# Two transformer blocks on one core: six raw weight buffers and five pairs of split ones instead of eight and four

## What is computed

```
x = first_block(x, ...)     # rms_norm; h @ w_in; three attentions; branches; w_out; MLP
x = second_block(x, ...)    # two layers over 256 tokens and 256 context tokens

# first_block
h = rms_norm(x, norm_mix)
(q, k, v of nsa, swa and moba, merge_gate) = split(h @ w_in)
o_a = nsa_attention(..., cmp_pos, cmp_w1, cmp_w2, bias)   # compressed, selected, window
o_b = banded_attention(..., swa_sinks)
o_c = moba_attention(...)
x = x + sum(sigmoid(merge_gate) * (branches @ w_branch)) @ w_out
h = rms_norm(x, norm_mlp)
x = x + square(relu(h @ w_mlp_in)) @ w_mlp_out

# second_block, for each of two layers
shift, scale, gate = split(silu(c) @ w_mod + b_mod)       # and the same of the context
u = (rmsnorm(x) * (1 + scale) + shift) @ w_in
x = x + gate * ((attentions(u) * silu(u_gate)) @ w_o)
```

## Time and profile before

| | us |
|---|---|
| three runs | 2912.19, 2914.12, 2914.35 |
| their median | 2914.12 |
| the profiled execution | 2914.6 |
| its span | 2912.8 |
| TensorE busy (PE) | 2882.0 |
| VectorE busy (DVE) | 1985.7 |
| ScalarE busy (ACT) | 1272.7 |
| GpSimd busy (POOL) | 225.5 |

### The profile page before, as it was taken

The page is one execution under the profiler, slowest core; times in us unless marked ns, Lnnn a source line. Parts: engine busy times, 40 slices in busy tenths (PEclk is TensorE's granted clock), DMA queues, the critical chain, the costliest instruction groups (busy, mean ns, idle before and its releaser), DMA issues. The chain is left out here.

```text
span 2912.8 us, 36839 instructions
## 1 busy us (share of the span) xinstructions
PE 2882.0 (99%) x13834; PEld 2378.1 (82%) x13834; DVE 1985.7 (68%) x2768; ACT 1272.7 (44%) x2101; POOL 225.5 (8%) x303
## 2 busy tenths in 40 slices
PE   9999999999999999999999999999999999999998
PEld 7898788888888888888888878777888888878877
DVE  6897466668879999999975844544534655676655
ACT  5443355553454444443555233333433325345543
POOL 1000000011002001010100000001000100112000
PEclk9999999999999999999999999999999999999999
DMA  8988956568768878878864744334333743776444
GB/s 288 296 306 275 330 163 192 152 202 284 253 212 275 281 263 283 279 252 291 274 211 138 230 154 139 123 116 135 116 125 123 250 162 109 260 225 212 133 136 154
DMA packets 307853, 612.07 MB, mean 210 GB/s; under 512 B 25916, under 2 KB 81689, under 8 KB 306781
## 3 DMA queue, kind: packets, MB, share of 16 engines
q1 hardware_dynamic: 288268, 545.79, 57.8%
q0 software_dynamic: 18176, 62.61, 6.0%
q10 hardware_dynamic: 1232, 1.33, 0.1%
HBM read 568.98 MB, written 41.84 MB: 210 GB/s over the span
## 5 line engine op out<-in xcount | busy, mean ns | idle before, releaser
L507 DVE TENSOR_TENSOR w_lo<-raw,w_hi 128x1024 fp32r<-128x1024 f32 (+3 forms) x778 | 934.2, 1213 | 266.5 <-ACT w_hi L501 260.7
L501 ACT ACTIVATE w_hi<-raw 128x1024 fp32r<-128x1024 f32 (+3 forms) x778 | 805.2, 1047 | 697.7 <-PE acc L737 536.9
L737 PE MATMUL acc<-w_hi,a_hi 128*128 128x512 f32 (+3 forms) x2024 | 785.4, 389 | 0.6 <-ACT stage L850 0.5
L737 PE MATMUL acc<-w_hi,a_lo 128*128 128x512 f32 (+3 forms) x2024 | 778.2, 385 | 0.0
L724 PE MATMUL acc<-w_hi,a_hi 128*128 128x512 f32 (+2 forms) x1328 | 538.0, 405 | 3.9 <-DVE w_lo L507 3.7
L737 PE MATMUL acc<-w_lo,a_hi 128*128 128x512 f32 (+3 forms) x2024 | 527.2, 385 | 0.0
L726 PE MATMUL acc<-w_hi,a_lo 128*128 128x512 f32 (+2 forms) x1328 | 517.9, 390 | 0.0
L725 PE MATMUL acc<-w_lo,a_hi 128*128 128x512 f32 (+2 forms) x1328 | 516.5, 389 | 0.0
L737 PEld LDWEIGHTS acc<-w_hi,a_hi 128*128 128x128 f32 x2024 | 380.0, 188 | 75.1 <-issue 3.3
L737 PEld LDWEIGHTS acc<-w_lo,a_hi 128*128 128x128 f32 x2024 | 378.2, 188 | 72.7
L737 PEld LDWEIGHTS acc<-w_hi,a_lo 128*128 128x128 f32 x2024 | 380.1, 188 | 70.0
(11 more groups left out here) (416 smaller groups left out, 2496.2 us busy)
## 6 DMA issues: line engine op xcount, KB each, us to landing
raw<-in_w_mod SPq DMA_DIRECT2D x192, 512.0 KB, 4.8
raw<-in_w_in SPq DMA_DIRECT2D x128, 512.0 KB, 5.1
raw<-in_w_mlp_in SPq DMA_DIRECT2D x128, 512.0 KB, 4.3
raw<-in_w_mlp_out SPq DMA_DIRECT2D x128, 512.0 KB, 5.6
raw<-in_e_w_in SPq DMA_DIRECT2D x104, 512.0 KB, 4.5
raw<-in_w_o SPq DMA_DIRECT2D x64, 512.0 KB, 6.0
raw<-in_o_w_in SPq DMA_DIRECT2D x64, 512.0 KB, 4.5
raw<-in_w_in SPq DMA_DIRECT2D x56, 448.0 KB, 4.6
```

What stands on the lines that cost most here:

```text
L501: nc.scalar.activation(w_hi[:, n % SPLITS, 0:size], raw[:, r % RAWS, 0:size], ACT.Copy)\
L507: nc.vector.tensor_tensor(w_lo[:, n % SPLITS, 0:size], raw[:, r % RAWS, 0:size], w_hi[:, n % SPLITS, 0:size].bitcast(F32), ALU.subtract)\
L737: return nc.tensor.matmul(acc[:, bank, 0:s.width], s.lhs(part, kt, tt), w, start=start, stop=False)
```

## The change

The ring of raw chunks has six buffers instead of eight, and the ring of split chunks five pairs instead of four. A raw buffer takes 4 KB of each partition, a pair of split ones 8 KB, so the memory taken stays the same and nothing behind it moves. No instruction is added or taken away. Everything that counts in RAWS or SPLITS follows: the waits of the loads and of the copies, the slots of the splits in the regions, and the places of the regions' loads.

```
--- before.py
+++ after.py
@@ -33,7 +33,7 @@
 GATE0 = 2560
 NCMP = (SEQ - 32) // 16 + 1
 NM = 3 * DM // P
-RAWS, SPLITS = 8, 4
+RAWS, SPLITS = 6, 5
 NEG = -1e30
 EPS = 1e-6
 TINY = 1e-30
```

## The result

The changed kernel took 2917.86 us in the median of 20 runs (2915.80 to 2919.68), the kernel before 2912.94 in as many (2912.19 to 2915.35). The ratio is 1.0016 with a 95% interval of 1.0010 to 1.0022: slower by 4.9 us. I had said 2913, a little down, and the range ended at 2922. The time is within 0.2% of the kernel before, but the direction is wrong. The profiled execution of the changed kernel took 2919.5 us, its span is 2917.7: 4.9 us over the span of before, the same distance as between the medians.

What follows compares the result with a forecast made beforehand. The prediction took TensorE as the bound, busy 2882.0 us of a span of 2912.8. It summed 2914.6 + 0 + 0 + 2.5 - 3.6 = 2913.5, less 0.5 to the median, to 2913 us, range 2907 to 2922.

Steps and rivals of the forecast that it cites:

- Part 1: Fifth pair of split buffers: no split moves, so 0; bounds all 3.7 us won, or nothing.
- Part 2: Six raw chunks in the first projection, the MLP and all later streams: loads still land in time, 0.
- the slower rival: First projection, 60 to 262 us: ring of six too short, 12.5 us lost, 2926; chance 0.10.
- Part 3: Compression rows, 274 to 314 us: chunks land behind a later release, TensorE stalls, +2.5 us; bounds 0 and 7.
- Part 4: Loads before the first attention: two raw chunks fewer ahead, keys up to 3 us sooner, sinks' stall covered, -3.6 us.
- my own case: Whole kernel: rows cost 2.5 us, sinks win 3.6, the rest 0; 2913, own range 2911 to 2918, chance 0.53.
- the rival between: Rows cost 2.5 us and the sinks' stall isn't relieved: 2917, or 2921.6 with 7 for the rows; chance 0.18.

Runs made afterwards that it cites:

- half rows: The changed kernel with only half of each compression row loaded (256 KB instead of 512): 2913.56 us, ratio 1.0004 to the kernel before.
- the run with a quarter of the context: The changed kernel with a quarter of the context's columns loaded by GpSimd at 773 us: 2917.68 us, ratio 1.0017 to the kernel before.

## Why the prediction was wrong

**Part 1, the fifth pair: right.** Taken at 0; added to six raw buffers, the pair moves the time by nothing that can be measured. What it takes from ScalarE's waits shows up in part as waits for landings.

**Part 2, the long streams: right for the first projection, incomplete for the rest.** With six chunks out the landings of 184 to 196 us took 6.8 us in place of 8.6, and TensorE stood nowhere: the slower rival fell on the point named against it. But I tested only whether TensorE gets its chunk in time. At 787 us the chunk was in time and VectorE's next work, the sum into `XR`, was not: +0.84. The place is the end of the output stage, which I didn't name: I went from the first projection to "the MLP and all later streams" and gave them 0. What failed is that step; the stage and the work queued behind the splits on VectorE belonged into it.

**Part 3, the rows: the mechanism was right, the size was not, and this decided the sign.** 2.5 us against 6.9 (4.9 to 6.9 in four profiles with six buffers and these rows), at the end of the bound of 7. The term that failed is this +2.5, and three things in its working were off. The first stall, 0.86 at 281.81, I hadn't followed: that chunk left at 269.07 before, ahead of the release of a row, and now stands behind it and leaves at 274.33. The chunk I gave 0.9 landed at 288.86, not 290.20, and cost nothing. And I kept the bursts at the times of the trace of before. But a stall ahead of a pair of rows delays the pair (286.43 to 287.52), the pair delays the release, the release delays the next burst (287.13 to 288.22), and that burst holds the next chunk: it came at 295.92, not 293.70, and cost 1.74. Half of these 2.2 us is the later issue (1.09); the other half is a longer landing (7.3 us in place of 6.1), which no run here takes apart. What a period loses is handed on to the next. I had this as the reason for the upper bound and left it out of the value.

**Part 4, the sinks: the stall went, but only in part by the chain that I gave, and the size came from an untypical execution.** The profile shows the stall and the slow clock gone, 3.3 us for a predicted 3.6. But I predicted the median, and 1.7 of the 3.6 were a slow clock that one profile of four has. A typical stall is worth 1.1 to 1.6 us. Subtracting the 0.5 us between that execution and the median was no cure: its excess sat in the very place that the change touches. And the chain was priced too high: the two raw chunks are worth 1.0 us of the keys' landing, not 3.0, and 0.4 us for the values' store, on which SyncE waited until 347.0 (I had read the keys' landing, 346.5). With TensorE on time (half rows) 1.06 us of the stall are left. The rest went only where TensorE came late out of the rows, which I hadn't forecast: that the wait was gone altogether was, as far as these runs show, luck, paid for by part 3. On the rule of the Trainium skill about taking turns ("DMA: Bandwidth & Descriptors", section "Queues, rings and completion order", as in the prediction): with eight buffers the keys' landing fell from 6.6 to 3.8 when only the loads of another queue were moved, so it doesn't run independently of them; a division of that 2.8 between the turns and the stores ahead on its own queue was not measured.

**The sum again** with what was measured: +4.9 to 6.9 (rows), +0.8 to 0.9 (`XR`), -1.1 to -1.6 (sinks, in an execution with full clock): +4.1 to +6.7, and 4.9 was measured.

**The rivals.** None of them is what happened; it was my own case with part 3 at its upper end and part 4 at a third of its value. The nearest in number is the rival between (2917), and half rows bear out a part of it: without a late TensorE the two raw chunks left most of a typical stall. Its condition, the stall still there, did not hold in the changed kernel.

No version beat both kernels clearly. The kernel before with the first region's loads behind four chunks is the lowest, 2911.5 us in both series, but within its interval it equals the kernel before.

## What to carry to other kernels

Where a buffer's release hangs on the engine that starves, a loss is handed on to the next period: follow the whole chain release, issue, landing, use with the new times, period by period, and don't subtract one from a fixed trace. When a ring gets shorter, look at everything that stands in order behind the delayed work on each engine, not only at the final consumer. And before a stall is priced from one profile, see in a second one whether its size and the clock behind it are the same.

## What the runs showed of the hardware that was not expected

A load of 2 MB on GpSimd's queue kept every raw chunk of SyncE's queue from landing for 7.5 us (8.7 before). The DMA queues of the changed kernel from 777 to 782 us, behind the context's load (packets, MB, share of the 16 engines):

```profile
q0 software_dynamic: 220, 1.65, 79.6%
q1 hardware_dynamic: 167, 0.34, 17.6%
```

Counted in packets of the profile the two queues get similar shares, 220 to 167. But GpSimd's packets are 7.5 KB in the mean (1.65 MB by 220) and SyncE's 2.0 KB, so in bytes it is nearly five to one. The Trainium skill, "DMA: Bandwidth & Descriptors", section "Queues, rings and completion order", has the engines take turns between queues packet by packet. This row is in keeping with it, but whether the profile's packets are those between which the engines turn is not shown.

The length of a wait did not decide TensorE's clock behind it. Behind the sinks it was 1.00 after waits of 1.14, 1.25 and 1.63 us, in the rows 1.00 after 1.74 us, and behind the sinks at the lower level after 1.85 and 4.25 us. But at the start of the kernel before the order is turned round: in the second profile TensorE waited 2.29 us and got 0.57 of the clock in the next 4 us, in the fourth it waited 2.69 us and got 1.00. Of each pair of rows the first is TensorE's timeline, the second the window behind it (granted clock third from the right):

```profile
17.25 1.04 PE L1118 MATMUL acc<-ident,XR 128*128 128x128 f32 x4 [2.29 <-DVE a_lo L1162]
17.25:21.25 4.00, 4.00 (x14) 3.66 (x15) 2.60 (x4) 3.10 (x7) 0.00 (x0) 0.57 1.06 383
```

```profile
17.37 0.63 PE L1118 MATMUL acc<-ident,XR 128*128 128x128 f32 x4 [2.69 <-DVE a_lo L1162]
17.37:21.37 4.00, 4.00 (x24) 3.73 (x25) 2.60 (x4) 3.10 (x7) 0.00 (x0) 1.00 1.06 385
```

And in the run with a quarter of the context the clock fell at 1969 us behind three waits of 0.28, 0.80 and 0.36 us, which the kernel before has as well, without a fall. So a short wait of TensorE can cost the clock in one execution and nothing in another, and a stall is to be priced with both.
